# Sample attention: half of the cached keys read from a second, turned copy of the cache

## The reference

```python
ckv_past = cache_ckv[j][page_table].reshape(bs, -1, R_KV)      # 8 x 4096 x 256
kpe_past = cache_kpe[j][page_table].reshape(bs, -1, D_ROPE)    # 8 x 4096 x 32
sp = (jnp.einsum('bqhr,bkr->bhqk', ql, ckv_past)
      + jnp.einsum('bqhd,bkd->bhqk', qp, kpe_past)) * MLA_SCALE
p = jax.nn.softmax(jnp.concatenate([sp, s], axis=-1), axis=-1)
o = jnp.einsum('bhqk,bkr->bqhr', p[..., :n_past], ckv_past) + ...
```

## Time and profile before

| | us |
|---|---|
| median of 3 runs (3503.6 to 3508.55) | 3503.63 |
| span of the profiled execution, first to last instruction | 3501.1 |
| two PEER layers, sum of the stretches 300 to 1642 and 2150 to 3501 | 2693 |
| `latent_projections`, 1642 to 1928 | 286 |
| `latent_sample`, 1928 to 2150 | 222 |

### The profile page before, as it was taken

The page is one execution under the profiler, slowest core; times in us unless marked ns, Lnnn a source line. Parts: engine busy times, 40 slices in busy tenths (PEclk is TensorE's granted clock), DMA queues, the critical chain, the costliest instruction groups (busy, mean ns, idle before and its releaser), DMA issues. The chain is left out here.

```text
span 3501.1 us, 34014 instructions
## 1 busy us (share of the span) xinstructions
PE 2983.7 (85%) x10561; PEld 1480.5 (42%) x10561; DVE 2185.4 (62%) x5266; ACT 1438.0 (41%) x4182; POOL 1301.9 (37%) x1112
## 2 busy tenths in 40 slices
PE   8987888888889888887999886888888888888886
PEld 7653333433334433333554764434333434433332
DVE  4874667666667766664362334666766676766765
ACT  3122445444444544443351222444444444544444
POOL 0211444444544444452001010445444454444442
PEclk9988999999999999999999897999999999999999
DMA  4015999999999999998203345999999999999998
GB/s 163 29 52 228 421 421 414 421 421 415 420 398 421 418 421 421 421 419 350 81 1 162 134 165 220 421 421 414 421 421 421 415 408 421 409 421 421 421 419 355
DMA packets 178372, 1194.53 MB, mean 341 GB/s; under 512 B 22320, under 2 KB 28240, under 8 KB 38150
## 3 DMA queue, kind: packets, MB, share of 16 engines
q0 software_dynamic: 154368, 1128.34, 77.8%
q1 hardware_dynamic: 22525, 63.11, 4.8%
q10 hardware_dynamic: 1296, 0.90, 0.1%
HBM read 1188.29 MB, written 4.46 MB: 341 GB/s over the span
## 5 line engine op out<-in xcount | busy, mean ns | idle before, releaser
L1581 PE MATMUL p_acc<-p_rows,p_diag 128*128 128x512 f32 (+1 forms) x4160 | 1973.0, 616 | 412.8 <-ACT p_diag L1184 411.0
L1414 DVE CUSTOM_DVE_ANT_0 p_rows<-p_rows,p_x_n 128x1024 f32<-128x1024 f32 x1024 | 1243.7, 1223 | 790.5 <-DMA p_rows<-in_peer_uv,p_ids 788.4
L1096 POOL DMA_INDIRECT p_rows<-in_peer_uv,p_ids x1024 | 1217.0, 1188 | 1384.6 <-PE p_acc L1581 1281.6
L1581 PEld LDWEIGHTS p_acc<-p_rows,p_diag 128*128 128x128 f32 (+1 forms) x4160 | 752.9, 192 | 1508.5 <-ACT p_diag L1184 790.8
L1178 ACT ACTIVATE p_acts<-p_dots 128x1 f32<-128x1 f32 x1040 | 208.3, 200 | 871.8 <-DVE p_dots L1414 870.4
L1184 ACT ACTIVATE p_diag<-ident,p_gated 128x128 f32<-128x128 f32 x1024 | 410.9, 401 | 33.6
L1180 ACT ACTIVATE p_gated<-p_acts,p_gates 128x1 f32<-128x1 f32 x1024 | 301.6, 295 | 33.2
L1531 PE MATMUL p_q_bank<-p_w_q,p_xT 128*128 128x256 f32 x1024 | 234.9, 383 | 2.2 <-ACT p_xT L1127 2.2
L1531 PEld LDWEIGHTS p_q_bank<-p_w_q,p_xT 128*128 128x128 f32 x1024 | 196.1, 192 | 55.5 <-issue 28.5
L1150 ACT COPY p_q_rows<-p_q_bank 128x256 f32<-128x256 f32 x68 | 25.2, 370 | 347.7 <-PE p_q_bank L1531 347.7
L1623 POOL DMA_INDIRECT smp_past<-in_cache_rows,smp_row_ids x32 | 30.0, 937 | 361.1 <-PE c_ps L2096 227.4
(11 more groups left out here) (402 smaller groups left out, 2483.0 us busy)
## 6 DMA issues: line engine op xcount, KB each, us to landing
p_w_q<-in_w_q_heads SPq DMA_DIRECT2D x16, 1024.0 KB, 12.2
p_rows<-in_peer_uv,p_ids POOLq DMA_INDIRECT x1024
a_w_in<-in_ab_w_in SPq DMA_DIRECT2D x6, 1024.0 KB
a_w_in<-in_ab_w_out SPq DMA_DIRECT2D x1, 4096.0 KB
c_arena<-in_c_w_out SPq DMA_DIRECT2D x1, 4096.0 KB, 12.7
smp_past<-in_c_w_out SPq DMA_DIRECT2D x1, 4096.0 KB
a_w_in<-in_ab_w_in SPq DMA_DIRECT2D x4, 1008.0 KB, 21.3
smp_past<-in_w_qx SPq DMA_DIRECT2D x1, 3072.0 KB, 18.6
```

The costliest lines, as they stand in the source:

```text
L1096: nc.gpsimd.indirect_dma_start(out=rows[:, slot % RING, :], out_offset=None, in_=w[f"peer_uv{layer}"], in_offset=bass.IndirectOffsetOnAxis ...
L1414: nc.vector.tensor_tensor_reduce(rows[:, k % RING, 0:D_MODEL], rows[:, k % RING, 0:D_MODEL], x, 1.0, 0.0, ALU.mult, ALU.add, dots[:, slot ...
L1581: last = nc.tensor.matmul(acc[done % 2][0:n, at], diag[:, slot // GROUP % 4, j, 0:n], rows[:, (slot + j) % RING, D_MODEL + 512 * b:D_MODEL ...
```

## The change

A second table is laid out on the host beside `cache_rows`: `cache_turned` has each page turned, 128 rows of 288 numbers (1152 bytes) per page, where a row belongs to a partition of the turned form (256 latent numbers as two halves of 128 lanes, and 32 rotary numbers as four parts). The second 16 pages of each sequence (keys 2048 to 4095) are gathered from it, in addition to the gather of all 32 pages from `cache_rows`, which the values need. One indirect DMA brings one page: 128 rows of 1152 bytes. There are 128 of them, in 16 pieces of 8, into a ring of three pieces `turned_c` (`TURNED_BUFS`). PE turns only the first four page groups and half of the rotary part; `scores(b, 1)` reads `turned_c` directly.

```diff
@@ latent_projections
-            for dst, name in ((table, "page_cols"), (spread, "spread"), (part, "sixteenth")):
-                sp.dma_start(dst[:], w[name]).then_inc(table_in, 16)
+            for dst, name in ((table, "page_cols"), (spread, "spread"), (part, "sixteenth"), (lane, "lane")):
+                sp.dma_start(dst[:, :], w[name]).then_inc(table_in, 16)
+            sp.dma_start(smp["turned_ids"][:], w["turned_pages"].to_broadcast([128, 128])).then_inc(table_in, 16)
...
-            dve.wait_ge(table_in, 48)
-            nc.vector.tensor_copy(table_f[:], table[:]).then_inc(table_ready, 1)
+            dve.wait_ge(table_in, 80)
+            nc.vector.tensor_copy(table_f, table[:]).then_inc(table_ready, 1)
+            nc.vector.tensor_copy(pages_f, smp["turned_ids"][:]).then_inc(pages_ready, 1)
+            dve.wait_ge(pages_ready, 1)
+            nc.vector.tensor_scalar(smp["turned_ids"][:], pages_f, 128.0, lane[:], ALU.mult, ALU.add)
@@ latent_sample, POOL
-            for b in range(BUFS, B):
-                pool.wait_ge(o_ps, b - BUFS + 1)
-                gather_past(nc, w, smp, b)
+            def gather_turned(piece):
+                if piece >= TURNED_BUFS:
+                    pool.wait_ge(s_ps, 2 * ((piece - TURNED_BUFS) // 2 + 1))
+                for k in range(KEYS_8):
+                    at = KEYS_8 * piece + k
+                    nc.gpsimd.indirect_dma_start(out=turned_c[:, piece % TURNED_BUFS, k, :], out_offset=None, in_=w["cache_turned"],
+                                                 in_offset=bass.IndirectOffsetOnAxis(ap=smp["turned_ids"][:, at:at + 1], axis=0)
+                                                 ).then_inc(turned_in[piece % TURNED_BUFS], 16)
+            for piece in range(TURNED_BUFS):
+                gather_turned(piece)
+            for b in range(B):
+                for piece in (2 * b + TURNED_BUFS, 2 * b + TURNED_BUFS + 1):
+                    if piece < 2 * B:
+                        gather_turned(piece)
+                if BUFS <= b + 2 < B:
+                    pool.wait_ge(o_ps, b)
+                    gather_past(nc, w, smp, b + 2)
@@ DVE
-                page_out(b, 5)
-                page_out(b, 6)
                 if b == 0:
                     self_out()
+                partial_max(b)
                 if b:
                     normed(b - 1)
-                partial_max(b)
@@ PE, scores
+                else:
+                    for piece in (2 * b, 2 * b + 1):
+                        pe.wait_ge(turned_in[piece % TURNED_BUFS], 16 * KEYS_8 * (piece // TURNED_BUFS + 1))
...
+                            nc.tensor.matmul(dst.rearrange("h (s g q) -> h s g q", s=NQ, g=KEYS_8), qlT[:, c, b, :], turned_slots(b, j, c), start=(c == 0), stop=False)
@@ PE, order
-                turn_pages(b, 4)
-                turn_pages(b, 5)
                 scores(b, 0)
                 if b:
                     turn_weights(b - 1)
-                turn_pages(b, 6)
-                turn_pages(b, 7)
+                scores(b, 1)
                 if b:
                     total_sums(b - 1)
                     weighted(b - 1)
-                scores(b, 1)
```

More of the change, by code:

```diff
@@ L2446, in turn_free @@
             def turn_free(i, b, half):
-                before = i - 4 if b == 0 and i == PT + 2 else i - 2
-                if before >= 0:
-                    pe.wait_ge(*turned(before, b, half))
+                if i == KPE or i == 2 and half == 1:
+                    if b:
+                        pe.wait_ge(*turned(4, b - 1, half))
+                elif i >= 2:
+                    pe.wait_ge(*turned(i - 2, b, half))
                 elif b:
-                    pe.wait_ge(*turned(before + TURNS, b - 1, half))
+                    pe.wait_ge(*turned(PT if b > 1 else 3, b - 1, half))
             def turn_rope(b):
-                for half in range(2):
-                    turn_free(KPE, b, half)
-                    for g in range(NQ * half, NQ * half + NQ):
-                        if g % 2 == 0:
-                            pe.wait_ge(past_in[b % BUFS][g // 2], 16 * (b // BUFS + 1))
-                        at = KEYS_8 * R_KV + 128 * (g % 2)
-                        last = nc.tensor.transpose(turn[0][:, 128 * g:128 * g + 128], past[:, b % BUFS, g // 2, at:at + 128], ident[:])
-                    last.then_inc(turn_ps, 1)
+                turn_free(KPE, b, 0)
+                for g in range(NQ):
+                    if g % 2 == 0:
+                        pe.wait_ge(past_in[b % BUFS][g // 2], 16 * (b // BUFS + 1))
+                    at = KEYS_8 * R_KV + 128 * (g % 2)
+                    last = nc.tensor.transpose(turn[0][:, 128 * g:128 * g + 128], past[:, b % BUFS, g // 2, at:at + 128], ident[:])
+                last.then_inc(turn_ps, 1)
             def turn_pages(b, g):
@@ L2472, in scores @@
             def scores(b, half):
-                for g in range(4 * half, 4 * half + 4):
-                    pe.wait_ge(*turned(GROUP_TURN[g], b))
+                if half == 0:
+                    for g in range(4):
+                        pe.wait_ge(*turned(GROUP_TURN[g], b))
+                else:
+                    for piece in (2 * b, 2 * b + 1):
+                        pe.wait_ge(turned_in[piece % TURNED_BUFS], 16 * KEYS_8 * (piece // TURNED_BUFS + 1))
                 pe.wait_ge(*turned(KPE, b))
@@ L2484, in scores @@
                         at = KEYS * half + 128 * a
[L2485 removed]
+                        dst = s_bank[group(j), at:at + 128]
+                        if half == 0:
+                            last = nc.tensor.matmul(dst, qpT[:, b, a, :], kpeT[:, j, :], start=False, stop=(a == NQ - 1))
+                        else:
+                            last = nc.tensor.matmul(dst.rearrange("h (g q) -> h g q", g=KEYS_8), qpT[:, b, a, :], turned_rope(b, j), start=False, stop=(a == NQ - 1))
                 last.then_inc(s_ps, 1)
@@ L2519, in weighted @@
             def weighted(b):
+                for piece in range(2, PIECES):
+                    pe.wait_ge(past_in[b % BUFS][piece], 16 * (b // BUFS + 1))
                 pe.wait_ge(*weights_turned(b))
```

70 lines of the change are left out of this document (45 added, 25 removed).

## The result

The changed kernel takes 3613.65 us (median of 4 runs, 3610.8 to 3615.0) against 3505.35 us for the kernel before: a ratio of 1.0307, 95% interval 1.0293 to 1.0322. It is slower by 108 us where 7 to 9 were forecast. The profiled execution has a span of 3612.9 us, 111.8 over that of before. The page shows what kind of loss it is: PE and POOL do about what was foreseen, and in the slices of the stage nobody is full.

What follows compares the result with a forecast made beforehand. PE's order of work bounded latent_sample; after the change POOL's gathers would. End +3.5, exposed `weighted` +4.5 and start +1.0 gave +9.0 us on a 3501.1 us span, forecast 3512 us; range 3501 to 3524, main case 3506 to 3522.

Steps and rivals of the forecast that it cites:

- the one on cover: In latent_sample, POOL asks for scores 6.9 us after PE has them, so stalls like 3.4 us are covered.
- The rival with this mechanism: In latent_sample, PE's signals are held while POOL issues gathers back to back: +108 us, 3612; chance 0.06.
- POOL's pitch: In latent_sample, POOL issues one gather every 1.243 us, also for the short rows of 1152 bytes.
- short rows are issued faster: Rival: POOL's gathers cost by bytes, 0.42 us each, and PE or DMA sets the pace: -38 us, 3466; chance 0.12.
- small gathers wait for each other's landing: Rival: POOL's 147 KB gathers run one behind the other, 2 us each: +114 us, 3618; chance 0.02.
- the 1.9 us of the upper bound: Upper bound for a short-row gather on POOL: 1.9 us or so, by which single PEER-layer gathers are lengthened.
- PE's 17.3 us a sequence: In latent_sample, a sequence would take 17.3 instead of 24.2 us if PE still set the pace.
- POOL as the bound at 24.9 us: In latent_sample, POOL's 20 gathers a sequence take 24.9 us, more than PE's 17.3, so POOL sets the pace.
- The end: End of latent_sample: last second scores 3.5 us later, then the moved `weighted` exposed for 4.5 us.
- the branch for which the text had 2128: End of latent_sample: if piece 15 of the turned pages comes last, beside `w_out`, scores end at 2128; 2124.5 was taken.
- The start of `latent_projections`: Two more loads on SP ahead of those DVE waits for: +1 us, bounds +0.4 and +2.
- 24.2 us each: Time of each of six sequences in latent_sample before the change, 145 us together, some 3 us stall in five sequences.

Runs made afterwards that it cites:

- b_wait: Kernel before, with POOL also waiting for the running sequence's second scores before its four past gathers: 3485.38 us, ratio 0.9939.
- after_again: The changed kernel, untouched, profiled again in a later session: 3624.69 us, ratio 1.0343 to the kernel before (3504.13 us).
- a_sp_split: Changed kernel, turned pages loaded in page order by SP (second half of keys wrong), past gathers cut into two pairs: 3468.18 us, ratio 0.9972.
- after_third: The changed kernel, untouched, in a session where the kernel before takes 3475.3 us: 3514.28 us, ratio 1.0107.
- b_split: Kernel before, POOL waiting for second scores, its four past gathers cut into two pairs, the second about 4.5 us later: 3477.43 us, ratio 0.9920.
- a_sp: Changed kernel, turned pages loaded by SP's plain loads in page order instead of POOL's gathers (second half of keys wrong): 3480.23 us, ratio 0.9933.
- a_dyn: Changed kernel, turned pages loaded by SP, which reads each page's row from the table into a register: 3511.74 us, ratio 1.0013.
- a_dyn2: Changed kernel, turned pages loaded by SP, a sequence's 16 table rows read into registers before the wait for scores: 3503.23 us, ratio 0.9994.

## Why the prediction was wrong

**The step that failed is the one on cover**: "6.9 us of slack cover stalls like that of 3.4 us". It took the stall of the earlier trace rows as a quantity of 3.4 us. It is no quantity but a condition, that can last as long as POOL's burst and up to 4.4 us more. All five cases of before had the same burst of four gathers, so they could not tell "3.4 us" from "until the burst ends"; the prediction had measured the second ("signals arrive 2.1 us after the last of them has begun") and then costed the first. With bursts of 16, 20 and 24 gathers it was up to 17, 22 and 30 us, against a slack of 6.9. The rival with this mechanism was named and priced at 3612, 2 us from the result, with a chance of 0.06. What was held against it, one sum of DVE on time at the end of a burst of 12 gathers, is one signal against five of five, and it could not bear the weight: in `b_wait` seven signals of one burst come on time before others are held, and in `after_again` one comes out inside the burst while the others stay. The signal at the end of the 12 gathers is on time in the changed kernel too (burst from 1874.18, its matmul ends 1887.78, it rises 1887.79), so the exception repeats, and no run explains it. The rival's working was near too: 42.2 us a round, for a burst of 20, where the trace of the result has 37.6 to 38.3 and that of `after_again`, with bursts of 20, 41.0 to 41.6.

**POOL's pitch**: right. The short rows take 0.95 us and come 1.25 us apart, as forecast from the earlier trace rows; the rival "short rows are issued faster" is out. So is "small gathers wait for each other's landing": where the queue was empty before them they land 2.4 to 2.8 us after their issue, with the next ones in flight. The section "Anatomy of one DMA — SWDGE (gpsimd) path" of the page DMA: Bandwidth & Descriptors of the Trainium skill gives such a transfer a fixed part of about 2.0 us; these 2.4 to 2.8 us agree with it. That time vanishes behind the pitch of issue. One reading was wrong without effect: the 1.9 us of the upper bound is about what single gathers of the PEER layers last (2.01 us at most), not what they are lengthened by.

**PE's 17.3 us a sequence**: right, 17.45 in `a_sp_split`, but for its one sequence of 27.8. POOL as the bound at 24.9 us: right where nothing is held, 24.98 in `after_third`, and the train of 148 lasts 184.8 us (forecast 184.0).

**The end**: near in sum by luck, wrong in its terms. In `after_third`, measured from the start of the stage, the second scores of sequence 7 end 9.3 us later than before (forecast 3.5): the last piece of turned pages comes last, at 2126.5, 11.8 us after its issue, beside `w_out`. This is the branch for which the text had 2128 and which it did not take. `weighted` in front of the last maximum costs 4.3 us (forecast 4.5). Against it stand 3.2 us in the rest of the tail, which no step foresaw: the two projections take 2.06 and 3.64 us where before they ran at half clock, 3.06 and 5.68. Together 10.4; forecast 8. (The terms named for the bounds of the forecast's own range give 3507.7 and 3519.5, not 3506 and 3522; nothing hangs on it.)

**The start of `latent_projections`**: forecast 1 us, measured 0.3 (from POOL's first memset there to its first in `latent_sample`: 285.5 us against 285.3), in `after_third` 0.7. DVE's wait for the loads grew from 2.75 to 3.34 us.

**The number 3512** holds where no signal is held (3514.28), but there the kernel before takes 3475, not 3504: 28 of its 3504 us were the stall that the earlier trace rows shows and that the prediction let stand as part of "24.2 us each". `b_split` agrees: with next to nothing held its stage is 28 us shorter than that of before. Undisturbed it is 19.8 us a sequence, which the earlier trace rows had for sequence 7. So the change costs 39 us in the one kind of session, of which an estimate from 25.0 us of POOL against 19.8 us of PE gives 31 for six sequences (before has no trace there), and 108 to 121 us in the other. The forecast counted POOL's train from the start of the stage, and no stall of before is in that; what it set beside it, 3504, had the hold in it. So the time fits one kind of session and the difference of 9 us neither. The sign was right, and stronger than the text had it: undisturbed, the kernel before leaves POOL 5 us a sequence less than its trace showed.

What would have shown it ahead: a cost of the stall in PE's window, sequence 2 against 7 in the earlier trace rows (24.4 against 19.8 us), puts 4.6 us a sequence on POOL's four gathers. A change that makes five times as many of them then has this price as its first suspect: in proportion 23 us a sequence, where the result has 37.8 us less the undisturbed 19.8, 18.

## What to carry to other kernels

A stall seen five times with the same burst behind it is one point and not yet a law: before it is put under slack, ask what it grows with, and price it at the size of the change. A transfer moved to POOL's indirect gathers costs 1.25 us of POOL per 128 rows (rows of 1152 to 9216 bytes here). Keep their bursts short (two at a time) and away from a signal on which the chain waits: in sessions with the hold one added wait on POOL brought the kernel before from 3505 to 3485 us, the split to 3477. Time the kernel before in every session, for one session's baseline doesn't hold for the next.

## What the runs showed of the hardware

- While POOL issues indirect gathers back to back, PE's semaphore signals can be held until up to 4.4 us after the last one (0.3 to 1.3 us for bursts of four), while PE's operations, and the signals of DVE and ACT, go on. Gathers do it; memsets of POOL and loads issued by SP don't. PE's signals were up to 17 us late behind bursts of 16, 22 us behind 20 and 30 us behind one of 24, and ACT and DVE waited for them. In its section "Who interferes with whom" the page SBUF — State Buffer of the Trainium skill says that PE and ACT never wait on anyone. It speaks of the ports to SBUF, and PE's operations here agree with it; but ACT stood 127.9 us in the stage, in five waits, for signals of PE that were held.
- In bursts of four, signals that follow each other within 0.6 us mostly pass for the first 3 us or so (in `a_sp` and `a_dyn` some of these were up to 1.8 us late, in `a_dyn2` up to 2.5); one that comes at 2.1 us after a silence of 2.4 does not. A gap of 0.54 us between two gathers is enough to let one out.
- The hold belongs to a session and not to a chip: one chip (the same number on record) had it in one session and not in another, with 3504 and 3477 us for the same kernel. What sets it in a session isn't settled by these runs; nor is the path on which PE's signals and POOL's gathers meet. A fetch of PE's instructions was ruled out as the trigger.
- A register read and an issue on SP take 1.1 to 1.3 us a load, about as much as a gather takes on POOL (1.25); the issue alone takes 0.51.
